# Expert value products turned over (256-column instead of 512-column products), and two operand placements moved

## The reference, cut to what matters

```
act = gelu(h @ u.T)              # h: 256 x 1024, u: 16384 x 1024
out = (gate * act) @ v           # gate: 256 x 16384, v: 16384 x 1024
x   = x + g2 * out
```

## Time and profile before

| | us |
|---|---|
| median of three runs | 3437.38 |
| lowest and highest | 3434.26, 3440.91 |
| the profiled execution's own time | 3439.32 |
| its span, first to last instruction | 3437.4 |
| TensorE busy | 3351.0 (97%) |
| VectorE busy | 2457.1 (71%) |
| mean granted TensorE clock | 0.987 |

### The profile page before, as it was taken

One profiled execution on the slowest core, in us unless ns is written; L12 is line 12 of the kernel. 1 busy time (PEld: TensorE's weight loads), 2 busy tenths in 40 slices (PEclk: granted clock), 3 DMA queues, 4 the chain that ended last, 5 costly groups with the idle time before them and its releaser, 6 DMA issues.

```text
span 3437.4 us, 69595 instructions
## 1 busy us (share of the span) xinstructions
PE 3351.0 (97%) x24630; PEld 3020.3 (88%) x24630; DVE 2457.1 (71%) x5105; ACT 1631.2 (47%) x3275; POOL 362.6 (11%) x480
## 2 busy tenths in 40 slices
PE   8999999999999999999999999999999999999998
PEld 7878889988888998889888888888889888888887
DVE  6744457765434877448998888887539998888887
ACT  4253356433434743145555555555446555555554
POOL 0212000020210010000550000000000640000000
PEclk9999999999999999899999999999999999999999
DMA  8733379874336985135348888888335258788885
GB/s 231 180 86 94 108 222 285 246 184 130 84 94 172 278 258 133 50 110 151 88 125 195 193 197 194 195 193 193 107 112 169 77 143 195 191 196 196 195 195 133
DMA packets 644022, 565.18 MB, mean 164 GB/s; under 512 B 62028, under 2 KB 589403, under 8 KB 643547
## 3 DMA queue, kind: packets, MB, share of 16 engines
q1 hardware_dynamic: 638564, 542.16, 60.7%
q0 software_dynamic: 4960, 19.93, 1.8%
q10 hardware_dynamic: 278, 0.08, 0.0%
HBM read 550.52 MB, written 9.44 MB: 163 GB/s over the span
## 4 chain that ended last, share of the span: by engine, by line
PE 83%; DVE 13%; ACT 2%; issue 1%; DMA 1%; POOL 0%; SPq 0%; DVEq 0%; ACTq 0%; POOLq 0%
PE bank L1479 15%; PE bank L862 14%; PE bank L884 14%; PE bank L1496 7%; PE bank L1499 7%; PE bank L1493 7%; PE bank L905 4%; PE bank L1454 2%; PE bank L858 2%; DVE uT L3367 2%; PE bank L1288 1%; PE bank L985 1%; DVE arena L3290 1%; DVE arena L3281 1%; DVE arena L3282 1%
## 5 line engine op out<-in xcount | busy, mean ns | idle before, releaser
L1479 PE MATMUL bank<-t_high,u_parts 128*128 128x256 f32 x3072 | 420.6, 279 | 1.3 <-ACT u_parts L2218 1.2
L1479 PEld LDWEIGHTS bank<-t_high,u_parts 128*128 128x128 f32 x3072 | 398.4, 188 | 20.4 <-ACT u_parts L2218 2.9
L3406 DVE TENSOR_TENSOR v_low<-ring,v_high 128x512 fp32r<-128x512 f32 x512 | 336.9, 690 | 59.3 <-ACT v_high L2230 35.2
L1496 PE MATMUL bank<-v_high,w_low 128*128 128x512 f32 x1024 | 322.3, 396 | 0.0
L1493 PE MATMUL bank<-v_high,w_high 128*128 128x512 f32 x1024 | 320.8, 394 | 1.0 <-ACT v_high L2230 1.0
L1499 PE MATMUL bank<-v_low,w_high 128*128 128x512 f32 x1024 | 321.8, 395 | 0.0
L2230 ACT ACTIVATE v_high<-ring 128x512 fp32r<-128x512 f32 x512 | 298.2, 618 | 38.2 <-PE bank L1499 38.2
L2218 ACT ACTIVATE u_parts<-bank 128x512 fp32r<-128x512 f32 x384 | 219.9, 594 | 191.7 <-DVE bank L3378 188.7
L1782 ACT ACTIVATE arena<-bank 128x256 f32<-128x256 f32 (+1 forms) x270 | 103.7, 387 | 414.4 <-PE bank L862 234.6
L862 PE MATMUL bank<-hT,ring 128*128 128x256 f32 (+2 forms) x1232 | 280.9, 385 | 6.1 <-DVE hT L2676 6.1
L862 PE MATMUL bank<-arena,ring 128*128 128x256 f32 (+2 forms) x1168 | 272.6, 388 | 5.6 <-DVE arena L3112 3.0
(11 more groups left out here) (477 smaller groups left out, 6361.9 us busy)
## 6 DMA issues: line engine op xcount, KB each, us to landing
ring<-in_peer_v SPq DMA_DIRECT2D x256, 512.0 KB, 4.6
ring<-in_peer_u SPq DMA_DIRECT2D x768, 128.0 KB, 4.3
ring<-in_w_in SPq DMA_DIRECT2D x128, 512.0 KB, 3.9
ring<-in_mlp_up SPq DMA_DIRECT2D x64, 512.0 KB, 4.8
uT<-in_mod_w SPq DMA_DIRECT2D x64, 512.0 KB, 5.3
ring<-in_mlp_down SPq DMA_DIRECT2D x64, 512.0 KB, 5.0
ring<-in_peer_u SPq DMA_DIRECT2D x64, 512.0 KB, 3.8
arena<-in_mod_w POOLq DMA_DIRECT2D x32, 512.0 KB, 4.9
```

Source lines behind the costliest of these rows:

```text
L1479: ins = eng.matmul(PB[6 + b][:, 0:S], u_parts[:, part, k * P:k * P + P], moving[:, k, :], start=(n == 0), stop=(n == len(products) - 1))
L1496: eng.matmul(PB[2 * tt + q][:, :], w_low[:, b, t], v_high[:, d], start=False, stop=False)
L3406: tt_(v_low[:, j % 4, d], ring[:, 2 + j % 4, d], v_high[:, d].bitcast(F32), ALU.subtract).then_inc(sem("vL_ready"), 1)
```

## The change

1. `combine` is turned over: the stationary operand is now a 128x128 chunk of `v_high` or `v_low`, the moving one all 256 tokens of `w_high` or `w_low`. 24 matmuls of 256 columns take the place of 12 of 512. Value columns are on the output's partitions, so the sums in banks 0 to 3 (two chunks of 256 columns in each) already have the layout of `xT`. Waits and counts stand where they stood.
2. At the end of a layer the copies to `moe_t`, the 16 turns and their semaphores go. DVE adds straight from banks 0 to 3, four chunks after the first half of the last combine and four after the second.
3. Because banks 0 to 3 are still being read then, the second layer's first tiles go to banks 5 to 7 and two norms use bank 4.
4. `mod` (384 bytes) is allocated ahead of `tab` and `wT`, which so lie 384 bytes further. As they are moving operands now and `selT` is stationary, moving is again 192 bytes ahead of stationary modulo 512.
5. For f == 1 (one tile in eight) both halves of `u_parts` lie 192 bytes further on, so that stationary and moving operand begin at the same place modulo 512 in that tile's score.

```diff
+        mod = sb("mod", [P, DEPTH, MOD])
         tab = sb("tab", [P, 2, 2, S])
         wT = sb("wT", [P, 2, S])
-        mod = sb("mod", [P, DEPTH, MOD])
...
-        u_parts = rounded("u_parts", "uT", 0, [P, 2, 1024])
+        u_lying = [[rounded(f"u_part{part}{aside}", "uT", 1024 * part + aside * AHEAD, [P, 1024]) for part in range(2)]
+                   for aside in range(2)]
+
+        def u_parts(f):
+
+            return u_lying[f == 1]
...
+        def raw_bank(label):
+
+            t = tiles[label][0]
+            return PB[(5 if label[0] == "c" else 0) + t % BANKS]
+
+        def expert_sum(c):
+
+            return PB[c // 2][:, (c % 2) * S:(c % 2) * S + S]
...
-                        d = slice(q * 512, q * 512 + 512)
+                        chunks = [(c, slice(c * P, c * P + P)) for c in range(4 * q, 4 * q + 4)]
                         eng.wait_ge(sem("wH_ready"), i * 8 + (j + 1 + base))
                         eng.wait_ge(sem("vH_ready"), i * 16 + (2 * j + q + 1 + 2 * base))
-                        for tt, t in enumerate(tokens):
-                            eng.matmul(PB[2 * tt + q][:, :], w_high[:, b, t], v_high[:, d], start=first, stop=False)
+                        for c, d in chunks:
+                            eng.matmul(expert_sum(c), v_high[:, d], w_high[:, b, :], start=first and c % 2 == 0, stop=False,
+                                       skip_group_check=True)
                         eng.wait_ge(sem("wL_ready"), i * 8 + (j + 1 + base))
-                        for tt, t in enumerate(tokens):
-                            eng.matmul(PB[2 * tt + q][:, :], w_low[:, b, t], v_high[:, d], start=False, stop=False)
+                        for c, d in chunks:
+                            eng.matmul(expert_sum(c), v_high[:, d], w_low[:, b, :], start=False, stop=False, skip_group_check=True)
...
-                eng.wait_ge(sem("v_free"), 2 * (base + NKEY))
-                for q in range(2):
-                    eng.tensor_copy(moe_t[:, 1, q * 512:q * 512 + 512], PB[2 + q][:, :]).then_inc(sem("experts1_ev"), 1)
                 if l == 0:
                     gains(1, 0, raw_c)
                 for k in range(KD):
-                    if k % 2 == 0:
-                        eng.wait_ge(sem("moe_mm"), dve.next("moe_mm"))
-                    stt_(xT[:, k, :], PB[4 + k // 2][:, (k % 2) * S:(k % 2) * S + S], mod[:, l, 40 + k:41 + k],
+                    if k % 4 == 0:
+                        eng.wait_ge(sem("v_free"), 2 * (base + NKEY) - 1 + k // 4)
+                    stt_(xT[:, k, :], expert_sum(k), mod[:, l, 40 + k:41 + k],
                          xT[:, k, :], ALU.mult, ALU.add).then_inc(sem("x_ready"), 1)
```

More of the change, by code:

```diff
@@ L1002, in raw_columns @@
                         tile_ready("raw_ready", base + k + 1)
-                        ins = eng.matmul(PB[t % BANKS][:, 0:S + 1], wv[:, k, :], raw[:, k, :], start=(k == 0), stop=(k == KD - 1))
+                        ins = eng.matmul(raw_bank(label)[:, 0:S + 1], wv[:, k, :], raw[:, k, :], start=(k == 0), stop=(k == KD - 1))
                     ins.then_inc(sem("unit_done"), 1)
@@ L1478, in score @@
                             eng.wait_ge(sem("h_split" if moving is t_low else "hH_ready"), H_PARTS * l + k // 2 + 1)
-                        ins = eng.matmul(PB[6 + b][:, 0:S], u_parts[:, part, k * P:k * P + P], moving[:, k, :],
+                        ins = eng.matmul(PB[6 + b][:, 0:S], u_parts(f)[part][:, k * P:k * P + P], moving[:, k, :],
                                          start=(n == 0), stop=(n == len(products) - 1))
@@ L1486, in combine @@
                         eng.wait_ge(sem("gate_ev"), 64 * (l + 1))
-                    tokens = [slice(tt * P, tt * P + P) for tt in range(TT)]
                     for q in range(2):
-                        d = slice(q * 512, q * 512 + 512)
+                        chunks = [(c, slice(c * P, c * P + P)) for c in range(4 * q, 4 * q + 4)]
                         eng.wait_ge(sem("wH_ready"), i * 8 + (j + 1 + base))
                         eng.wait_ge(sem("vH_ready"), i * 16 + (2 * j + q + 1 + 2 * base))
-                        for tt, t in enumerate(tokens):
-                            eng.matmul(PB[2 * tt + q][:, :], w_high[:, b, t], v_high[:, d], start=first, stop=False)
+                        for c, d in chunks:
+                            eng.matmul(expert_sum(c), v_high[:, d], w_high[:, b, :], start=first and c % 2 == 0, stop=False,
+                                       skip_group_check=True)
                         eng.wait_ge(sem("wL_ready"), i * 8 + (j + 1 + base))
-                        for tt, t in enumerate(tokens):
-                            eng.matmul(PB[2 * tt + q][:, :], w_low[:, b, t], v_high[:, d], start=False, stop=False)
+                        for c, d in chunks:
+                            eng.matmul(expert_sum(c), v_high[:, d], w_low[:, b, :], start=False, stop=False, skip_group_check=True)
                         eng.wait_ge(sem("vL_ready"), i * 16 + (2 * j + q + 1 + 2 * base))
-                        for tt, t in enumerate(tokens):
-                            ins = eng.matmul(PB[2 * tt + q][:, :], w_high[:, b, t], v_low[:, j % 4, d], start=False, stop=last)
+                        for c, d in chunks:
+                            ins = eng.matmul(expert_sum(c), v_low[:, j % 4, d], w_high[:, b, :], start=False,
+                                             stop=last and c % 2 == 1, skip_group_check=True)
                         ins.then_inc(sem("v_free"), 1)
@@ L1513, in expert_tiles @@
                 combine(15, 7, last=True)
[L1514 to L1522, removed]
             def gdn(l, fill):
@@ L1716, in _ @@
                 else:
-                    raw_columns([("c", j) for j in range(RAW)], raw_c, 3)
+                    raw_columns([("c", j) for j in range(RAW)], raw_c, 4)
                     for j in range(RAW, 6):
@@ L1749, in _ @@
                 expert_tiles(l)
-            norm_sum(0)
+            norm_sum()
             norms[0] += 1
@@ L2694, in raw_out @@
                 t = tiles[label][0]
-                ps, col = PB[t % BANKS], small[:, 44:45]
+                ps, col = raw_bank(label), small[:, 44:45]
                 eng.wait_ge(sem("unit_done"), last_unit(label))
```

16 lines of the change are left out of this document (6 added, 10 removed).

## The result

| | before | changed |
|---|---|---|
| median of 12 runs, us | 3435.45 | 3444.12 |
| lowest and highest | 3426.69, 3440.91 | 3438.79, 3448.7 |
| the profiled execution's own time | 3439.32 | 3441.32 |
| its span | 3437.4 | 3439.5 |

The ratio is 1.0025, 95% interval [1.0017, 1.0032]: 5.8 to 11 us slower, where 27 us faster was forecast.

A forecast was written before the change was run, and what follows sets the result against it. TensorE's matmul pace was taken to bound the expert loop. Terms -32.3 + 4 + 7 - 5.3 = -26.6 us gave 3412.7 against the profiled 3439.3, or 3411 us as median; range 3402 to 3434.

The forecast's parts named there:

- The step that failed: Expert loop: the 192-byte shift at f == 1 was taken to bring the short pace, 113.3 ns, as 128 bytes had.
- The term of -32.3 us: Expert loop: all 336 matmuls of an iteration at 113.3 ns, 38.07 us against 39.08, times 32 iterations.
- rival (b): Expert loop: long pace everywhere, 117.8 ns per matmul, +16.0 us less 5.3 at layer ends, 3448 us; chance 0.09.
- That the pace is a state: Expert loop: TensorE stays at 113.3 or 117.8 ns per 256 columns; a stall can leave it in either.
- Rival (a): Expert loop: paces stay mixed, mean 115.6 ns, -7.7 us in the loop, 3424 us with layer ends; chance 0.11.
- The combine turned over: Combine: 24 matmuls of 256 columns take 2.72 or 2.83 us per tile, -0.64 or +0.24 us for eight tiles.
- Rival (c): Expert loop: twice as many combine matmuls cost something each; at 4.5 ns each, +13.8 us, 3446 us; chance 0.05.
- The waits: Loop's start: TensorE waits 0.1 to 0.15 us per iteration, +4 us; long stretches after such stalls add +7 us.
- Rival (d): Expert loop: other engines bound it, both double combines waiting 0.3 us, 19 us lost in all, 3419 us; chance 0.06.
- Layer ends: End of each layer: sums of squares follow the last combine without the former gap, -5.3 us for both layers.
- Banks: Banks 4 to 7 in place of 0 to 2 and 3: no count changes and no cost.
- Rival (e): Expert loop: placement does nothing, scores keep an even mix and combine runs at it, 115.6 ns, 3424 us; chance 0.03.

The follow-up runs named there:

- e2: Changed kernel with the u rows of f == 1 shifted by 128 bytes in place of 192: 3410.17 us, ratio 0.9923.
- e9: Changed kernel with f == 1 shifted by 128 bytes and f == 4 by 192: 3428.75 us, ratio 0.9981.
- e1: Changed kernel without part 5, the u rows of f == 1 lying where all others lie: 3437.8 us, ratio 1.0011.
- e6: Changed kernel with f == 1 shifted by 128 bytes only in the first iteration of each layer: 3441.95 us, ratio 1.0026.
- e3: Changed kernel with `mod` allocated behind `wT` as before, so combine has distance 320 and the score 192: 3429.88 us, ratio 0.999.
- e10: Changed kernel with the u rows of f == 1 shifted by 256 bytes in place of 192: 3444.56 us, ratio 1.0023.
- e4: Kernel before with part 5 alone, 192 bytes at f == 1 and 512-column combines kept: 3433.34 us, ratio 1.0001.
- e7: Kernel before with the u rows of f == 1 shifted by 128 bytes, 512-column combines kept: 3437.39 us, ratio 1.0013.

## Why the prediction was wrong

**The step that failed** is "I take the short end as basis, since in rows 6 the displaced buffer was followed by the short pace; that its 192 bytes act like 128 is no row's". They do not in this loop: with 128 bytes (e2) it is short, with 192 it is long, and e9 shows 192 locking a short loop. The term of -32.3 us became +17.6, which is rival (b)'s +16.0 with 0.05 us more per iteration for the displaced score at 120.0 ns. Nor is the lock all of it: without the displaced tile (e1) a wait in a layer's first iteration makes the loop long, and nothing frees it. The earlier trace rows were evidence for 128 bytes alone, and a chance of 0.09 for (b) was far too low for a step with no row of its own.

**That the pace is a state** was right, and that a stall can leave it in either: e2 and e6 show both paces at the same instructions of one kernel. Rival (a) names in its aside that leaving a displaced buffer need not work one way only; e9 shows that, though no alternation from one iteration to the next came of it.

**The combine turned over** costs nothing by itself: 2.72 or 2.83 us for its 24 matmuls, as put. Rival (c) falls (with e2 an iteration has as many matmuls and takes 38.40 us). The formula of the Trainium skill's "TensorE: Matmul & The Clock Gate", "Back-to-back issue gap", gives 109.2 ns for 256 columns, for a matmul by itself; the prediction put it on a stream of them, where that section itself says that the formula miscounts. Measured are 113.3 and 117.8.

**The waits** did not come in the changed kernel, as TensorE was too slow for them. They came in e2, mostly ended by ACT's `v_high`: 19 of the 30 at the second combine of the pair at the loop's start, where the prediction had put them, and 11 at the second combine of the other pair. Behind the layers' first iterations 58 start intervals above 125 ns at L1506 exceed 113.3 by 6.7 us together, where 4 was forecast. The long intervals measured 1,910 x 4.5 ns = 8.6 us, forecast 7. That these are close is luck: a fifth of the waits turned the pace and not half, while the stretches of 204 to 264 matmuls from the other pair of combines on were longer than the 96 put. Rival (d)'s 19 us is out.

**Layer ends:** -5.5 us measured, -5.3 forecast (its own rows add up to 5.4). **Banks:** from the first layer's sums of squares to the second layer's first score are 386.8 us, before 389.5; the difference is within the scatter of such stretches, and no cost shows.

**The sum with 128 bytes:** -32.3 + 6.7 + 8.6 - 5.5 = -22.5; the profiled execution of e2 took 3418.45 against 3439.32, -20.9, and the 1.6 us between them no term tells; the medians differ by 24.5. The forecast of 3411 was thus nearly e2's 3410, the time of another kernel, and its terms for the loop fit that kernel alone. Rival (e), that placement does nothing, falls: 64 bytes less of it (e2) moved the time by 34 us. The Trainium skill's "SBUF — State Buffer", "SBUF: two separate sides", has TensorE's ports waiting on nobody. No run here looks at whether another engine's accesses hold them up; where its own two operands lie does change its pace.

**Left open.** Why some distances free the loop, one passes unnoticed and one locks it (and yet is followed by the short pace in e3), is not settled. No run here looks at the reads of the operands, or parts them from what other engines read and write at the time, and the list of distances (128, 64, 384 free, 448 neutral, 0 locks, 320 long always in the combine) gives no order that I could have used to foretell e10. Which waits turn the pace is open too, and so is whether it was the wait of 0.35 us or the displaced score behind it that turned the second layer of the changed kernel to the long pace.

## What to carry to other kernels

Where TensorE is never idle and yet scores of the same form differ in length, read the pace from the start times and treat it as a state: a displacement of one operand in one tile per iteration can be worth nearly 3% of the loop (38.54 against 39.63 us), or cost it a pace that it had (e9), and each value has to be run. Look at the loop's first wait too: in e1 it set the pace of all that followed. A precedent at one distance says nothing for another. When a forecast rests on such a step, give the opposite outcome a chance of the same order.

## What the runs showed of the hardware that was not expected

- At granted clock 1.00, 256-column matmuls follow each other every 113.3 or 117.8 ns, and each is kept for long (e6: short for 162 us, to 1940.06, then long for over 450).
- A wait of some 0.2 us can end the short pace (e6 at 1940.06), but need not: in e2 6 of 30 did, of the waits at 2936.52 and 2975.24 only the first. A stall can end the long pace as well (e1 at 1774.98).
- A tile displaced by 192 bytes runs at 120.0 ns, slower than either pace, and leaves the long one behind it where combines and scores have one distance. With the combines at distance 320 (e3) the scores behind it are short.
- A displacement of 256 bytes is not seen in the pace: that tile takes 2.83 us like its neighbours in a long loop, and leaves a short one short.
- Between 512-column matmuls (233.2 ns) the scores go on changing pace by turns, with either displacement tried (e4, e7).
